# Moving two gate tiles of a hybrid encoder step from the attention stage into a twelfth block pair

## The reference

```python
z = x @ w_in                      # 1024 x 6416, among its columns 24 tiles of 128 for the merge gates gl
log_a = log_sigmoid(ga @ w_gla_a2 + b_gla_a) / 16
o_a = rms_norm(gla_chunked(...)) * silu(gr)     # branch A, linear attention, 4 heads of 128
o_b = swa_banded(q, k, v, sinks)                # branch B, 8 heads of 64, window of own chunk + 2, with sinks
o_c = mem_attention(mq, mem_k, mem_v)           # branch C, 4 heads of 128 into 256 memory rows
g_a, g_b, g_c = split(sigmoid(gl + b_gate), 3)
mix = (g_a * (o_a @ w_br_gla) + g_b * (o_b @ w_br_swa) + g_c * (o_c @ w_br_mem)) @ w_o
x = layer_norm(ALPHA * x + mix);  x = layer_norm(ALPHA * x + conv_ffn(x))
```

## Time and profile before

| | us |
|---|---|
| median of 3 executions | 1728.0 (1724.7 to 1728.62) |
| profiled execution, its own time | 1725.59 |
| its span | 1723.8 |
| PE busy in the span | 1696.0 (98%) |
| PE weight load busy | 1637.0 (95%) |
| DVE busy | 1144.6 (66%) |
| ACT busy | 774.9 (45%) |
| POOL busy | 308.1 (18%) |

### The profile page before, as it was taken

How to read it: one execution, slowest core, us unless ns; L and a number is a source line. 1 busy time by engine, 2 the same in 40 slices (tenths; PEclk the granted TensorE clock), 3 DMA queues, 4 the chain that set the end, 5 groups by cost and what they waited for, 6 DMA issues and landing times.

```text
span 1723.8 us, 32867 instructions
## 1 busy us (share of the span) xinstructions
PE 1696.0 (98%) x12437; PEld 1637.0 (95%) x12437; DVE 1144.6 (66%) x1671; ACT 774.9 (45%) x1493; POOL 308.1 (18%) x399
## 2 busy tenths in 40 slices
PE   9999999999999999999999999999999999999997
PEld 8999999999999799889997889999999999999997
DVE  6656552565754766657656698777777777777686
ACT  6433332444443555564332155445544545544552
POOL 0144441000001200000000104333333332000023
PEclk9999999999999999999999999999999999999999
DMA  5565658422426411114465433222222222788532
GB/s 167 162 220 198 206 208 273 156 80 71 154 78 196 136 51 46 50 61 143 135 185 204 122 77 97 75 74 74 74 75 86 85 74 87 269 306 250 195 112 89
DMA packets 194839, 232.70 MB, mean 135 GB/s; under 512 B 22037, under 2 KB 144214, under 8 KB 194742
## 3 DMA queue, kind: packets, MB, share of 16 engines
q1 hardware_dynamic: 186534, 201.66, 37.4%
q0 software_dynamic: 8208, 29.72, 4.9%
HBM read 170.69 MB, written 60.07 MB: 134 GB/s over the span
## 4 chain that ended last, share of the span: by engine, by line
PE 62%; DVE 4%; issue 2%; ACT 1%; DMA 1%; SPq 1%; POOL 1%; POOLq 0%; ACTq 0%; DVEq 0%
PE banks L1792 24%; PE banks L1847 12%; PE banks L1266 5%; PE banks L1268 5%; PE banks L1267 5%; PE banks L1725 4%; PE banks L1562 1%; PE banks L1579 1%; PE banks L1574 1%; PE banks L1542 1%; PE banks L1547 1%; DMA kpad<-gates_scratch 1%; DVE wo L2965 0%; PE banks L1758 0%; DVE ln_st L3028 0%
## 5 line engine op out<-in xcount | busy, mean ns | idle before, releaser
L1266 PE MATMUL banks<-act_hi,w_hi 128*128 128x352 f32 (+1 forms) x672 | 224.6, 334 | 4.4 <-ACT gate_st L2067 2.1
L1792 PE MATMUL banks<-x_free_r,a_hi 128*128 128x256 f32 x1232 | 226.7, 282 | 2.0 <-ACT x_free L2405 1.5
L1268 PE MATMUL banks<-act_hi,w_lo 128*128 128x352 f32 (+1 forms) x672 | 218.5, 325 | 0.0
L1267 PE MATMUL banks<-act_lo,w_hi 128*128 128x352 f32 (+1 forms) x672 | 218.4, 325 | 0.0
L1792 PEld LDWEIGHTS banks<-x_free_r,a_hi 128*128 128x128 f32 x1232 | 190.2, 188 | 2.7 <-issue 2.0
L1792 PE MATMUL banks<-xs_hi,a_hi 128*128 128x274 f32 x616 | 178.8, 290 | 2.0 <-DVE xs_lo L3102 1.4
L1792 PE MATMUL banks<-xs_lo,a_hi 128*128 128x274 f32 x616 | 178.4, 290 | 0.0
L1792 PE MATMUL banks<-xs_hi,a_lo 128*128 128x274 f32 x616 | 178.3, 289 | 0.0
L1847 PE MATMUL banks<-b_hi,d_hi 128*128 128x238 f32 (+1 forms) x616 | 177.4, 288 | 0.3 <-DVE b_lo L3232 0.3
L1847 PE MATMUL banks<-b_hi,d_lo 128*128 128x238 f32 (+1 forms) x616 | 176.6, 287 | 0.0
L1847 PE MATMUL banks<-b_lo,d_hi 128*128 128x238 f32 (+1 forms) x616 | 176.4, 286 | 0.0
(11 more groups left out here) (364 smaller groups left out, 4332.6 us busy)
## 6 DMA issues: line engine op xcount, KB each, us to landing
w_raw<-in_w_in SPq DMA_DIRECT2D x80, 256.0 KB, 3.7
b_raw<-h_keep SPq DMA_DIRECT2D x77, 265.0 KB, 4.1
gate_in<-gates_scratch SPq DMA_DIRECT2D x24, 529.0 KB, 3.7
h_keep<-conv SPq DMA_DIRECT2D x22, 530.0 KB, 2.8
gates_scratch<-zu SPq DMA_DIRECT2D x11, 1058.0 KB, 7.3
s_buf<-in_w_down POOLq DMA_DIRECT2D x11, 1024.0 KB, 5.3
s_keep<-s_buf POOLq DMA_DIRECT2D x22, 512.0 KB, 6.8
w_raw<-in_w_up SPq DMA_DIRECT2D x44, 256.0 KB, 4.0
```

The lines of the kernel that those rows point to most:

```text
L1266: pe.matmul(out, hi, b_hi, start=start, stop=False)
L1267: pe.matmul(out, hi, b_lo, start=False, stop=False)
L1268: return pe.matmul(out, lo, b_hi, start=False, stop=stop)
L1792: last = pe.matmul(out, a[j][:, k, :], x[s][j][:, k, :], start=fresh and k == 0 and n_ == 0, stop=k == 3 and n_ == 2, skip_group_check=True)
```

## The change

`NZ` goes from 11 to 12: the new pair takes the gate tiles 22 and 23 (`Z_GATES` has a fifth entry, 22). Since the last pair now has the other parity, the dense slices behind it go to the other two PSUM banks, and one more window is written out at the end of the loop on PE, ACT and DVE. Stage B has six gate tiles left, that is 18 slices or 144 row blocks, and each of the same 24 steps takes 6 of these (18 matmuls in place of 24), so that a slice ends in the middle of a step, in 18 of the 24 steps. ACT evacuates a slice in the step where it ends, and ACT and DVE split the next tile in the step in which a tile ends, every fourth in place of every third. The loops over the middle rounds are written out. SP stores and loads two tiles less there, and the counts of semaphores and tile numbers behind stage B are moved to match.

```diff
-NZ = 11
+NZ = 12
+Z_LAST = (NZ - 1) % 2
-Z_GATES = (12, 14, 6, 8)
+Z_GATES = (12, 14, 6, 8, 22)
+ATT_UNITS = 6
+    def att_units(i, j):
+        first = (6 * i + j - 3) * ATT_UNITS
+        return [divmod(u, KD) for u in range(first, first + ATT_UNITS)]
+    def att_fill(i, j):
+        ends = [s for s, k in att_units(i, j) if k == KD - 1 and s >= 0]
+        return ends[0] if ends else None
...
-        last = gate_loop(T_GATE_B // 2, 16, 4, gate_st2, PS_GATE_B)
+        last = gate_loop(T_GATE_B // 2, 16, 3, gate_st2, PS_GATE_B)
...
-        z_pair(NZ - 1, 0)
+        z_pair(NZ - 2, 0)
+        z_pair(NZ - 1, Z_LAST)
...
         def gate_slice_b(i, j, beside=None):
-            if j % 3 == 0:
-                tile_start(i + (T_GATE_B // 2 + j // 3 - 1), 1 - j // 3)
-            proj_slice(i * 6 + (PS_GATE_B + j - 3), (PS_GATE_B + j - 3) % 2, 1 - j // 3, j % 3, beside)
+            for n_, (s, k) in enumerate(att_units(i, j)):
+                slot, (c, w) = s // 3 % 2, GROUPS[s % 3]
+                out = bank((PS_GATE_B + s) % 2)[:, 0:w]
+                if k == 0:
+                    if s % 3 == 0:
+                        tile_start((T_GATE_B + s // 3) // 2, slot)
+                    pe.wait_ge(q.proj_free, PS_GATE_B + s - 1)
+                last = product(out, w_hi[slot][:, k, :], w_lo[slot][:, k, :], act_hi[:, k, c:c + w], act_lo[:, k, c:c + w],
+                               k == 0, k == KD - 1)
+                if k == KD - 1:
+                    last.then_inc(q.proj_done, 1)
+                if beside and n_ in beside:
+                    beside[n_]()
...
-        with pe.Fori(1, NT // 2 - 1) as i:
+        for i in range(1, NT // 2 - 1):
             att_steps(i, False, False)
...
         def gate_out_b(i, j):
-            gate_out(i * 6 + (PS_GATE_B + j - 3), (PS_GATE_B + j - 3) % 2, j % 3, gate_st2, i * 2 + (1 + NFILL + j // 3))
+            s = att_fill(i, j)
+            if s is not None:
+                gate_out(PS_GATE_B + s, (PS_GATE_B + s) % 2, s % 3, gate_st2, 2 + NFILL + s // 3)
+        def next_gate(i, j):
+            s = att_fill(i, j)
+            if (i, j) == (0, 2):
+                split_hi(T_GATE_B // 2, 1)
+            elif s is not None and s % 3 == 2:
+                split_hi((T_GATE_B + s // 3 + 2) // 2, s // 3 % 2)
...
-                if j % 3 == 2:
-                    split_hi(i + (T_GATE_B // 2 + b), 1 - b)
+                next_gate(i, j)
```

More of the change, by code:

```diff
@@ L85 @@
 T_GATE_B = T_MQ + 10
-T_MERGE = T_MQ + 18
-T_WO = T_MQ + 30
-T_FFN = T_MQ + 38
+T_MERGE = T_MQ + 16
+T_WO = T_MQ + 28
+T_FFN = T_MQ + 36
 PW0, PW1, PBG, PW2, PCB, PGN, PHI = 0, NF * 2, NF * 4, NF * 4 + 24, NF * 6 + 24, NF * 8 + 24, NF * 8 + 25
@@ L505, in program @@
     BRANCHES = (2, 0, 1)
-    PS_Z, PS_G, PS_GA, PS_FILL, PS_MQ, PS_MQ_B, PS_MK, PS_MV, PS_GATE_B, PS_END = 6, 9, 11, 15, 57, 60, 63, 65, 67, 91
+    PS_Z, PS_G, PS_GA, PS_FILL, PS_MQ, PS_MQ_B, PS_MK, PS_MV, PS_GATE_B, PS_END = 6, 9, 11, 15, 57, 60, 63, 65, 67, 85
     q = Semaphores(sem)
@@ L594, in raw_count @@
         if par:
-            return 384 if isinstance(c, int) and c < 2 else c * 32 + 352
+            return 448 if isinstance(c, int) and c < 2 else c * 32 + 416
         return 32 * (W0 + 1) if isinstance(c, int) and c < 2 else c * 16 + 32 * (W0 + 1)
@@ L617, in program @@
     b_landed = [raw_b_landed, gate_landed[0], gate_landed[1], gate_stored[0], gate_stored[1], gate_stored[2]]
-    B_BASE = (raw_count(LAST, 1), 192, 192, 16 * (10 + NFILL), 16 * (10 + NFILL), 16 * (10 + NFILL))
+    B_BASE = (raw_count(LAST, 1), 192, 192, 16 * (8 + NFILL), 16 * (8 + NFILL), 16 * (8 + NFILL))
     B_RAWS = (1, 2, 1, 2, 1, 0, 0, 1, 1)
@@ L912, in _ @@
         merge_tile(T_MERGE // 2, 1, BRANCHES[1], 0)
-        last(3, (0,))
+        last(2, (0,))
         sp.wait_ge(q.staged, 2 * NT + 2)
@@ L916, in _ @@
         gate_back(0)
-        last(3, (1,))
+        last(2, (1,))
         for s in range(3):
-            sp.wait_ge(gate_stored[s], 16 * (10 + NFILL))
+            sp.wait_ge(gate_stored[s], 16 * (8 + NFILL))
         for k in range(12):
@@ L1384, in _ @@
         z_pair(1, 1, 1)
-        with pe.Fori(1, NZ // 2) as i:
+        with pe.Fori(1, (NZ - 1) // 2) as i:
             z_pair(i * 2, 0)
             z_pair(i * 2 + 1, 1)
-        z_pair(NZ - 1, 0)
+        z_pair(NZ - 2, 0)
+        z_pair(NZ - 1, Z_LAST)
         tile_start(1, 0)
@@ L1393, in _ @@
         for gi in range(3):
-            proj_slice(PS_Z + gi, 3 + 4 * (gi % 2), 0, gi)
+            proj_slice(PS_Z + gi, bank_a(1 - Z_LAST, gi % 2), 0, gi)
         for s in range(2):
@@ L2049, in _ @@
         z_window(1, 1)
-        with act.Fori(1, NZ // 2) as i:
+        with act.Fori(1, (NZ - 1) // 2) as i:
             z_window(i * 2, 0)
             z_window(i * 2 + 1, 1)
+        z_window(NZ - 2, 0)
         for k in range(3):
             for s in range(2):
-                z_snap(NZ - 1, 0, s, k)
+                z_snap(NZ - 1, Z_LAST, s, k)
         split_hi(1, 0, used=(q.prod_mm[1], z_count(NZ - 1, 0)))
         for s in range(2):
-            z_snap(NZ - 1, 0, s, 3)
+            z_snap(NZ - 1, Z_LAST, s, 3)
         split_hi(1, 1, used=(q.prod_mm[1], z_count(NZ - 1, 4)))
@@ L2070, in _ @@
         for gi in range(3):
-            gate_out(PS_Z + gi, 3 + 4 * (gi % 2), gi, gate_st, 0)
+            gate_out(PS_Z + gi, bank_a(1 - Z_LAST, gi % 2), gi, gate_st, 0)
             if gi == 1:
@@ L2242, in _ @@
         att_steps(0, True, False)
-        with act.Fori(1, NT // 2 - 1) as i:
+        for i in range(1, NT // 2 - 1):
             att_steps(i, False, False)
@@ L2294, in _ @@
         for gi in range(3):
-            act.wait_ge(gate_stored[gi], 16 * (10 + NFILL))
+            act.wait_ge(gate_stored[gi], 16 * (8 + NFILL))
         act.wait_ge(q.k_turned, 1)
@@ L2728, in _ @@
         z_window(1, 1)
-        with dve.Fori(1, NZ // 2) as i:
+        with dve.Fori(1, (NZ - 1) // 2) as i:
             z_window(i * 2, 0)
             z_window(i * 2 + 1, 1)
+        z_window(NZ - 2, 0)
         for k in range(3):
             for s in range(2):
-                z_combine(NZ - 1, 0, s, k)
+                z_combine(NZ - 1, Z_LAST, s, k)
             if k == 0:
@@ L2937, in att_steps @@
                     split_lo(T_GATE_B // 2, 0)
-                if j % 3 == 2:
-                    split_lo(i + (T_GATE_B // 2 + j // 3), 1 - j // 3)
+                s = att_fill(i, j)
+                if (i, j) == (0, 2):
+                    split_lo(T_GATE_B // 2, 1)
+                elif s is not None and s % 3 == 2:
+                    split_lo((T_GATE_B + s // 3 + 2) // 2, s // 3 % 2)
         def branch_lo(place):
@@ L2949, in _ @@
         att_steps(0, True, False)
-        with dve.Fori(1, NT // 2 - 1) as i:
+        for i in range(1, NT // 2 - 1):
             att_steps(i, False, False)
```

## The result

The changed kernel takes 1731.57 us (median of 8 runs, 1730.25 to 1736.37), the kernel before, timed beside it, 1725.76 (8 runs, 1724.58 to 1728.62): a ratio of 1.0038 [1.0027, 1.0049], or +5.8 us. The whole interval lies above 0.2%, the prediction's bound for a change that can be told from none. A second series (12 runs) gave 1732.04 against 1726.91: 1.0030 [1.0018, 1.0042]. The forecast was +6.4.

What follows compares the result with a forecast made beforehand. PE bounds the block pairs; in the attention PE and a serial DVE and ACT ring are in balance. +20.65 (pair) - 14.0 (attention) - 0.2 (dense slices) = +6.4 us, forecast 1733, range 1727 to 1738.

Steps and rivals of the forecast that it cites:

- The pair, +20.65: Stage of block pairs: one more pair costs PE's own pace, 168 matmuls at 0.123 us, +20.65 us.
- The boundary behind the pairs, -0.2: Dense slices behind the block pairs: PE's wait of 0.22 us at 280.05 goes, -0.2 us.
- A to B: Attention, from step j % 3 = 1 to 2: stays 7.05 us between masks, 0.97 us saved becomes PE's wait.
- B to C: Attention, from step j % 3 = 2 to 0: PE decides, 7.79 us between mask starts against 7.12 for DVE and ACT.
- C to A: Attention, from step j % 3 = 0 to 1: PE decides, 6.09 us between mask starts against 5.30 for DVE and ACT.
- The losses: Attention's 24 steps: 9.4 us of the 23.4 by PE's count are lost, so it gives 14.0 us.
- The estimates of 1.2 for the splits and 0.6 for the first step: Attention: tile splits every fourth step lose 1.2 us; the first filled step loses 0.6, its values waiting for DVE's copy.
- the ring: Attention, DVE and ACT: serial mask and reduction, four exponentials, four scalings, copy, next mask; 7.05 us in one step.
- The tail, 0.92 to 1.9: Attention's end: PE's wait ahead of the products with the values grows from 0.92 to about 1.9, 1.0 us lost.
- that rival: Attention: waits of 0.9 us a cycle let PE's clock fall; ten microseconds cost about five: 1738, chance 0.03.
- The loops: Attention's middle rounds written out: priced at 0, between 0 and +1.8 us.
- The rival by PE's count: Attention: PE alone decides, the full 23.4 us is given back, -3.0 us in all, 1722.6 or 1725.0; chance 0.12.

Runs made afterwards that it cites:

- the fastest kernel: The changed kernel with DVE's new order, the tail's first branch split moved, and 6, 5, 7 row blocks (6, 6, 6 in the tail): 1718.04 us, 0.9954 of before.
- The reordering: Changed kernel with 4, 8, 6 row blocks in the last three steps, DVE normalising k+1 after copy k and mask and reduction k+2: 1721.85 us, 0.9974 of before.
- the one with 0.92 of it: The changed kernel with its last three attention steps filled by 4, 8, 6 row blocks in place of 6, 6, 6: 1726.79 us, 1.0013 of before.

## Why the prediction was right, and where it was right by luck

The forecast was +6.4 and the runs say +5.8 and +5.1. Its central step is shown; its sum also holds two terms of the wrong size, offset by a third that it had put at nothing.

- **The pair, +20.65.** The snapshots are 20.65 apart, and PE's stretch to 480.92 is longer by 17.7, which is 20.65 less what the boundary gave.
- **The boundary behind the pairs, -0.2: mis-sized.** It gave 2.9 between these two executions: of PE's waits of 0.22, 0.17 and 1.90 none is left, and the starts behind them move by 2.9 in all. That is the upper end. The other profiled executions with eleven pairs have shorter waits there, 0.31 and 1.29 with the attention alone, 0.26 and 0.69 with the loops written out, and by the same starts they would give 1.9 and 1.3. I had taken the stretch behind 280.05 to move along as it is, and looked at its first wait alone. In the kernel before ACT's evacuation of a gate (gate_st) waits there for the landing of stores, 6.1 us for POOL's s_keep and 11.2 for its own; with the twelfth pair it waits 5.7 for its own and not for POOL's. The pair alone has the change, the attention alone hasn't. That the stores land before the pairs end, and so no longer meet the small loads behind them, is the likely mechanism; it was argued and not tested.
- **A to B stays at 7.05.** It is 7.05 and 7.06. The slack that I called nil was a little below it: by the fastest kernel's rows PE already waited some 0.14 us ahead of the memory values, unmarked. B to C is 7.76 (7.79 said, with 0.13 for waking PE where its own row, 653.13 - 653.02, gives 0.11), C to A 6.08 (6.09), the cycle 20.90 (20.93). The wait is 0.95 in cycles without a split in C. The reordering shows that it is the ring: with it gone, the cycle is PE's count.
- **The losses.** Up to the turning that opens the tail the count of PE gives 21.4 (22 steps of 0.974), the losses ahead of the tail were said to be 8.4, so 13.0 was to be given. The rows give 0.9 + 13.3 = 14.2. The estimates of 1.2 for the splits and 0.6 for the first step were 1.2 too large together: the first filled step waits 0.47 us, and where a split stands in C the wait in B is just shorter (0.68), so the two losses share their time.
- **The tail, 0.92 to 1.9.** 1.87, and 9.01 behind the turning, as before. The first merge product was to come at 774.1 and came at 774.50.
- **That product is on time by two errors.** The boundary, the splits and the execution's start (-1.0, a scatter) brought PE to the tail's wait 4.8 us earlier than said, and the lower clock took it back. I had named that rival (the waits bring the clock down: 1738) with a chance of 0.03 only, because the clock had stayed at 1.00 with loads idle for a tenth of the stage. But the many waits of 0.95 don't do it, for the clock stays at 1.00 through them in every profiled execution; it falls at the one of 1.87. Without its 7.0 us (6.0 against before, and the 0.97 that the last step was to give) the profiled execution would be +1.8 and not +8.8.
- **What the clock is worth in the median.** By the account above, the change without it costs +1.8, from one execution of each kernel, whose start and boundary alone scatter by 1 to 2 us. The kernel without the tail's wait should then be at -0.1 and is at -0.5 [-2.6, +1.6]; the one with 0.92 of it should be at +0.9 and is at +2.2 [+0.3, +4.1]. Both intervals hold these values, so of the measured +5.8 some 2 to 4 us are the clock's, as an estimate. That the change is slower by over 0.2% hangs on it: without the tail's wait, the ring kept, the ratio is 0.9997, no change that can be measured.
- **The loops.** 0 was right. The Trainium skill (Runtime: NRT & Kernel Launch, Instruction fetch mechanics) says that a taken branch outside the fetched window stalls, by which writing the loops out could only gain; 1.0000 [0.9990, 1.0011] shows no gain here.
- **The rival by PE's count** (1722.6 or 1725.0) fell: DVE is busy for 0.63 and ACT for 0.51 of the attention's stretch and they bound a third of its steps all the same. The Trainium skill (Perfetto Trace Analysis, Identifying the Most-Contended Engine) says to take the engine of the highest occupancy first and would have pointed to TensorE alone. The -3.0 that follows lies just inside what was measured once the order on DVE was changed (0.9974 is -4.5 [-6.4, -2.8]), and not before.

Left open: PE's wait ahead of the turning of the memory's keys (L1544),

```profile
575.64 1.09 PE L1544 MATMUL banks<-ident,mk_rows 128*128 128x128 f32 x8 [1.82 <-ACT mk_rows L2192]
```

which the execution of before doesn't have (its form with the loops written out has one of 0.71). It is 1.82 here, 3.38 in the second series and 0.35 to 3.07 in the other executions with the changed attention or the twelfth pair, for keys that a DMA brings and ACT splits. In the account it is offset by 3.4 us at half clock that the execution before has at 515. No run tells what sets its length.

## What to carry to other kernels

Before work is taken from a full engine inside a software pipeline, follow the other engines once around their own ring (here mask, exponentials, scalings, copy) and compare its length with the step. If both are equal, the saving turns into waits, and their busy shares of 0.6 and 0.5 do not tell you. Look first for an operation in the ring that nobody needs yet: moving the scalings behind the next unit's mask cost nothing and gave 6.7 us. And a single long wait of the matmul engine can cost several times its length in clock (1.87 us here, with 17 us at half clock behind it in both profiled executions): put filling where the longest wait is, not evenly.

## What the runs showed of the clock

The lower level of 1.2 GHz came with the tail's wait in each of the four profiled executions in which PE waited there for 1.27 us or more (1.87 twice for some 17 us, 1.87 in the attention alone for some 3.4, 1.27 for some 10), and in none of the eight in which it waited there for 0.92 or less. That is no rule for a wait's length: 1.82 and 2.05 us ahead of the memory keys were followed by full clock, 2.31, 3.04, 3.07 and 3.38 at the same place went with a fall. Nor does every fall have such a wait: the kernel before and the attention alone have 3.4 us at the lower level at about 515, and the fastest kernel has them at about 533, with 0.67 the longest marked wait in the 35 us ahead.

And the clock differs between executions of one kernel. Eight of the 20 of the changed kernel have a mean clock of 0.992 or 0.993, among them both profiled ones with their 17 us, and a ninth has 0.994; of the 142 other executions whose clock is on record, of nine other kernels, none is below 0.994. These nine take on average 4 to 5 us more than the rest (1735.1 against 1730.9, 1735.5 against 1730.6). What decides in which execution the long fall comes, no run tells. One profile alone, here one of the long ones, overstated the loss by 3 us.
